# Two of eight token tiles of a product-key retrieval FFN read the expert table as 128 blocks instead of gathering rows

## The reference

```python
q = (xb @ w_query).astype(jnp.float32).reshape(T, PEER_HEADS, 2, PEER_HALF)
scores = jnp.einsum('thpd,hpkd->thpk', q, sub_keys.astype(jnp.float32))
s_top, i_top = lax.top_k(scores, PEER_TOPK)
...
gate = jax.nn.softmax(best, axis=-1)
u_e = expert_down[idx]
v_e = expert_up[idx]
act = jax.nn.gelu(jnp.einsum('thkd,td->thk', u_e, xb).astype(jnp.float32), approximate=False)
return jnp.einsum('thk,thkd->td', (gate * act).astype(xb.dtype), v_e)
```

## Time and profile before

| | |
|---|---|
| median of 3 runs | 2949.64 us (2945.9 to 2950.95) |
| profiled execution | 2951.25 us, its span 2949.5 us |
| busy share PE, DVE, ACT, POOL | 67%, 65%, 41%, 39% |
| DMA | 1181.83 MB, 401 GB/s mean over the span |
| granted TensorE clock, mean | 0.70 of 2.4 GHz |

### The profile page before, as it was taken

How to read it: one execution, slowest core, us unless ns; L and a number is a source line. 1 busy time by engine, 2 the same in 40 slices (tenths; PEclk the granted TensorE clock), 3 DMA queues, 4 the chain that set the end, 5 groups by cost and what they waited for, 6 DMA issues and landing times.

```text
span 2949.5 us, 37543 instructions
## 1 busy us (share of the span) xinstructions
PE 1973.1 (67%) x12770; PEld 899.5 (30%) x12770; DVE 1914.2 (65%) x4707; ACT 1205.3 (41%) x3855; POOL 1148.5 (39%) x1032
## 2 busy tenths in 40 slices
PE   5788888887977466666665656566666666566553
PEld 4454453443534122232322312132222223232110
DVE  4776656665766366677576766677576766666544
ACT  1245444354454243444344443444344444444333
POOL 0043333333444244444444444444444444444332
PEclk9888987988988567666567557665666656666555
DMA  9599999999999999999999999999999999999997
GB/s 404 198 372 402 371 387 395 384 417 389 420 418 372 381 419 420 421 411 421 420 421 421 410 420 419 418 406 421 420 413 420 409 415 418 414 409 417 421 421 293
DMA packets 176213, 1181.83 MB, mean 401 GB/s; under 512 B 19731, under 2 KB 28947, under 8 KB 42774
## 3 DMA queue, kind: packets, MB, share of 16 engines
q0 software_dynamic: 147456, 1073.81, 88.9%
q1 hardware_dynamic: 28566, 105.63, 9.2%
HBM read 1170.98 MB, written 8.39 MB: 400 GB/s over the span
## 4 chain that ended last, share of the span: by engine, by line
DMA 52%; PE 23%; DVE 13%; ACT 7%; issue 3%; SPq 1%; POOL 1%; DVEq 0%; ACTq 0%; POOLq 0%
DMA work<-experts,expert_rows 40%; DMA weights<-experts,expert_rows 9%; PE ps_sum L750 7%; DVE work L1294 5%; PE ps_small L719 4%; PE ps_m L668 3%; PE ps_wide L694 2%; PE ps_m L632 2%; PE ps_m L612 2%; ACT weight L931 1%; DMA work<-w_ada 1%; ACT diag L936 1%; DMA h_next<-x_scratch 1%; DVE weights L1294 1%; ACT act_out L929 1%
## 5 line engine op out<-in xcount | busy, mean ns | idle before, releaser
L564 POOL DMA_INDIRECT work<-experts,expert_rows x836 | 933.0, 1116 | 1470.0 <-PE ps_sum L750 1295.1
L1294 DVE CUSTOM_DVE_ANT_0 work<-work 128x1024 f32<-128x1024 f32 x836 | 1020.7, 1223 | 666.8 <-DMA work<-experts,expert_rows 665.6
L750 PE MATMUL ps_sum<-work,diag 128*32 128x256 f32 x6688 | 750.0, 534 | 674.3 <-ACT diag L936 670.9
L929 ACT ACTIVATE act_out<-act_in 128x1 f32<-128x1 f32 x1024 | 207.5, 203 | 1228.1 <-DVE act_in L1294 1224.8
L750 PEld LDWEIGHTS ps_sum<-work,diag 128*32 128x32 f32 x6688 | 154.6, 127 | 1162.6 <-ACT diag L936 1095.3
L936 ACT ACTIVATE diag<-const,weight 128x32 f32<-128x32 f32 x1024 | 329.1, 321 | 33.6
L1294 DVE CUSTOM_DVE_ANT_0 weights<-weights,work 128x1024 f32<-128x1024 f32 x188 | 230.1, 1224 | 153.3 <-DMA weights<-experts,expert_rows 152.9
L564 POOL DMA_INDIRECT weights<-experts,expert_rows x188 | 212.5, 1130 | 299.6 <-PE ps_sum L750 289.7
L931 ACT ACTIVATE weight<-gate,act_out 128x1 f32<-128x1 f32 x1024 | 301.7, 295 | 33.2
L750 PE MATMUL ps_sum<-weights,diag 128*32 128x256 f32 x1504 | 176.1, 555 | 203.8 <-ACT diag L936 196.4
L694 PE MATMUL ps_wide<-h_cur,const 32*128 32x512 f32 x260 | 211.4, 904 | 0.8 <-ACT work L903 0.8
(11 more groups left out here) (159 smaller groups left out, 1717.6 us busy)
## 6 DMA issues: line engine op xcount, KB each, us to landing
work<-sides SPq DMA_DIRECT2D x68, 576.0 KB, 8.1
work<-w_ada SPq DMA_DIRECT2D x12, 2048.0 KB, 23.8
work<-experts,expert_rows POOLq DMA_INDIRECT x836, 16.2
weights<-sides SPq DMA_DIRECT2D x12, 576.0 KB, 36.8
weights<-w_in SPq DMA_DIRECT2D x3, 2048.0 KB, 17.8
x_buf<-x SPq DMA_DIRECT2D x8, 512.0 KB, 11.2
weights<-w_out SPq DMA_DIRECT2D x2, 2048.0 KB, 37.0
x_scratch<-h_buf SPq DMA_DIRECT2D x8, 512.0 KB, 7.8
```

Of the source, the lines that this page charges most:

```text
L564: nc.gpsimd.indirect_dma_start(ring[x.ring], None, experts, bass.IndirectOffsetOnAxis(ap=rows_flat[:, x.column:x.column + 1], axis=0),).th ...
L750: last = nc.tensor.matmul(ps_sum[quarter(c), x.group, :], diag[:, x.ring, :], ring[x.ring][:, D + c * QCOLS:D + (c + 1) * QCOLS], start=x. ...
L929: nc.scalar.activation(act_out[:, s:s + 1], act_in[:, s:s + 1], ACT.Gelu).then_inc(s_gelu, 1)
L1294: nc.vector.tensor_tensor_reduce(down, down, h2_spread[x.segment % 2], 1.0, 0.0, ALU.mult, ALU.add, act_in[:, x.g % TURN:x.g % TURN + 1]). ...
```

## The change

**What it does.** Tiles 2 and 3 (`DENSE`) no longer gather. The six other tiles (`LEGS`) keep their 128 slots each, 768 in all. For the two tiles the 16384 experts are read once, as 128 blocks of 1.05 MB (all experts with the same second key; a plain DMA from an array laid out for it, issued by POOL into the same ring). A block takes 8 matmuls of 256 columns for the down products of all 256 tokens (`down`), a Gelu over 128 x 256 (`gelu_block`), a multiplication with the map (`gate_block`) and 4 matmuls of 512 columns (`up`), which add into four banks. Block b stands at slot 494 + b x 254 / 128, so that about every two slots hold one, up to slot 750.

**The map of gates** has one number for each of the 256 tokens and 16384 experts, 16.8 MB. For each token POOL makes two one-hot rows with the token's 128 choices on the partitions (`make_onehots`, two operations of 128 columns), PE multiplies them (`map_bank`), ACT copies four tokens at a time (`copy_map`), SP stores 16 tokens at a time in pieces of 512 bytes (`store_map`) and reads the map back in 16 parts of 1.05 MB (`load_map`). This is placed at slots 324 to 388 and 430 to 494.

**What else moves.** The ring gets 13 buffers from slot 296 on (6 before that). All 128 sides are streamed, none is held. The turns stand closer: 26 of the 32 begin before slot 494. Steps 4, 11, 12 and 13 of a turn use one wide DVE operation where there were two or four. The mixer ends at slot 293. The mixer's tiles now share one piece of memory, that the map and the blocks use afterwards. After the last block, at slot 752 and 757, DVE finishes the two dense tiles (`dense_end`).

```diff
+LEGS = (0, 1, 4, 5, 6, 7)
+DENSE = (2, 3)
+LAST_SLOT = len(LEGS) * SLOTS
+BLOCKS = KEYS
+DENSE_TOKENS = len(DENSE) * P
+
+
 RING_MIX = 6
-RING = 8
-MIX_TILES = 2
-LATE_SLOT = 268
-LATE_ORDER = (6, 7, 4, 5, 0, 1, 2, 3)
+RING = 13
+LATE_SLOT = 296
+LATE_ORDER = tuple(range(RING_MIX, RING)) + tuple((LATE_SLOT + i) % RING_MIX for i in range(RING_MIX))
+DIAGS = 8
 
...
-MIX_AT = {1: -MIX_HEAD, 2: 31, 3: 70, 4: 109, 5: 150, 6: 190, 7: 230}
+MIX_AT = {1: -MIX_HEAD, 2: 34, 3: 76, 4: 132, 5: 174, 6: 216, 7: 259}
...
+TURN_AT = {(0, 0): None, (0, 1): 2, (0, 2): 22, (0, 3): 42, (1, 0): 70, (1, 1): 88, (1, 2): 106, (1, 3): 126,
+           (2, 0): 175, (2, 1): 192, (4, 0): 209, (4, 1): 226, (2, 2): 243, (4, 2): 260, (4, 3): 277, (2, 3): 294,
...
-ROUTE_STEPS = 19
-EXP_SLOT, MOVE_SLOT = 11, 19
-SIDES_BEFORE = (20, 15, 10, 5)
-ROUTE_AT = [None, 2, 28, 50, 74, 98]
-for _t in range(1, TILES):
-    ROUTE_AT += [SLOTS * _t + s for s in (2, 28, 68, 94)][:2 if _t == TILES - 1 else 4]
...
-
-BATCHES = [((0,), (1,), (2,), (3,))] + [((0, 1), (2, 3))] * (TILES - 1)
...
+MAP_KEYS = 8
+MAP_PARTS = KEYS // MAP_KEYS
+MAP_STORE = 16
+MAP_BANK = 4
+MAP_BANKS = P // MAP_BANK
+
+TURN_CHOICES_AT = [TURN_AT[t, PAIRS - 1] + MOVE_SLOT + 1 for t in DENSE]
+MAP_MADE_AT = [g + 14 for g in TURN_CHOICES_AT]
+MAP_TOKENS = 2
+MAP_BACK = 6
+
+DENSE_FROM, DENSE_SLOTS = 494, 254
+DOWN, GELU, GATED_D, UP = 1, 2, 3, 4
+DENSE_END = 752
 
...
+class Block:
+
+
+    def __init__(self, b):
+        self.b, self.g = b, DENSE_FROM + b * DENSE_SLOTS // BLOCKS
...
+def fill_ring(table, blocks):
+
+    fills, last, late = [0] * RING, [None] * RING, 0
     for x in table:
-        fills[x.ring] += 1
-        x.fill, x.before = fills[x.ring], last[x.ring]
-        last[x.ring] = x.g
-    return table, starts
+        for y in [x] + [block for block in blocks if block.g == x.g]:
+            if x.g < LATE_SLOT:
+                y.ring = x.g % RING_MIX
+            else:
+                y.ring, late = LATE_ORDER[late % RING], late + 1
+            fills[y.ring] += 1
+            y.fill, y.before = fills[y.ring], last[y.ring]
...
+            def store_map(i, n):
+                banks = MAP_STORE // MAP_BANK
+                if n % banks == banks - 1:
+                    store = (MAP_BANKS * i + n) // banks
+                    sp.wait_ge(s_map_sb, MAP_BANKS * i + n + 1)
+                    sp.dma_start(map_dram[:, :, store, :].rearrange("a p x -> p a x"),
+                                 map_store[store % 2]).then_inc(s_map_st[store % 2], 16)
+
+            def load_map(part):
+                if part < 2:
+                    for i in range(2):
+                        sp.wait_ge(s_map_st[i], 16 * (DENSE_TOKENS // MAP_STORE // 2))
+                else:
+                    sp.wait_ge(s_gated_d, MAP_KEYS * (part - 1))
...
+            def make_onehots(i, token):
+
+                bank = (P * i + token) // MAP_BANK
+                if token % MAP_BANK == 0:
+                    pool.wait_ge(s_numbers, 16)
+                    pool.wait_ge(s_choices, i + 1)
+                    if bank >= 2:
+                        pool.wait_ge(s_map_ps, bank - 1)
+                first, second = (onehot[bank % 2][:, e, token % MAP_BANK, :] for e in range(2))
+                nc.gpsimd.tensor_scalar(first, numbers, choices_t[:, 0, token:token + 1], None, ALU.is_equal)
+                nc.gpsimd.tensor_scalar(second, numbers, choices_t[:, 1, token:token + 1],
+                                        choices_t[:, 2, token:token + 1], ALU.is_equal, ALU.mult).then_inc(s_onehot, 1)
+
+            for x in TABLE:
+                gather(x)
+                for i, at in enumerate(MAP_MADE_AT):
+                    for token in range((x.g - at) * MAP_TOKENS, (x.g - at + 1) * MAP_TOKENS):
+                        if 0 <= token < P:
+                            make_onehots(i, token)
+                for block in blocks_at(x.g):
+                    wait_free(pool, block)
+                    nc.gpsimd.dma_start(ring[block.ring], blocks[block.b]).then_inc(s_row[block.ring], 16)
...
+            def map_bank(i, n):
+
+                bank = MAP_BANKS * i + n
+                pe.wait_ge(s_onehot, MAP_BANK * (bank + 1))
+                if bank >= 2:
+                    pe.wait_ge(s_map_sb, bank - 1)
+                else:
+                    pe.wait_ge(s_x1, TILES)
+                for token in range(MAP_BANK):
+                    last = nc.tensor.matmul(ps_map[bank % 2][:, token * KEYS:(token + 1) * KEYS],
+                                            onehot[bank % 2][:, 0, token, :], onehot[bank % 2][:, 1, token, :],
+                                            start=True, stop=True)
+                last.then_inc(s_map_ps, 1)
+
+            def down(block, queries_done, sides_done):
+
+                pe.wait_ge(s_row[block.ring], 16 * block.fill)
+                pe.wait_ge(s_q_sb, queries_done)
+                pe.wait_ge(s_score_sb, sides_done)
+                if block.b:
+                    pe.wait_ge(s_gelu_d, block.b)
+                else:
+                    pe.wait_ge(s_h2_d, 2)
+                    pe.wait_ge(s_wide_sb, WIDE_USE["turn", DENSE[1], 1] + 1)
+                weights_of = ring[block.ring][:, 0:D].rearrange("p (k e) -> p k e", k=KC)
+                for k in range(KC):
+                    last = nc.tensor.matmul(ps_d, weights_of[:, k, :], h2_d[:, k, :], start=(k == 0), stop=(k == KC - 1))
+                last.then_inc(s_down, 1)
+
+            def up(block):
+                pe.wait_ge(s_gated_d, block.b + 1)
+                if block.b == 0:
+                    pe.wait_ge(s_map_sb, MAP_BANKS * len(DENSE))
+                for i in range(len(DENSE)):
+                    for half in range(2):
+                        last = nc.tensor.matmul(ps_dense[i][half], gated_d[block.b % 2][:, i * P:(i + 1) * P],
+                                                ring[block.ring][:, D + half * HALF:D + (half + 1) * HALF],
+                                                start=(block.b == 0), stop=(block.b == BLOCKS - 1))
+                last.then_inc(s_block, 1)
...
+                for block in blocks_at(x.g - DOWN):
+                    down(block, queries_done, sides_done)
+                    downs += 1
+                for block in blocks_at(x.g - UP):
+                    up(block)
...
+            def copy_map(i, n):
+                bank, banks = MAP_BANKS * i + n, MAP_STORE // MAP_BANK
+                store = bank // banks
+                act.wait_ge(s_map_ps, bank + 1)
+                if store >= 2:
+                    act.wait_ge(s_map_st[store % 2], 16 * (store // 2))
+                at = bank % banks * MAP_BANK * MAP_KEYS
+                target = map_store[store % 2][:, :, at:at + MAP_BANK * MAP_KEYS].rearrange("p a (t k) -> p t a k", k=MAP_KEYS)
+                nc.scalar.copy(target, ps_map[bank % 2][:, :].rearrange("p (t a k) -> p t a k", t=MAP_BANK, k=MAP_KEYS)
+                               ).then_inc(s_map_sb, 1)
+
+            def gelu_block(block):
+                act.wait_ge(s_down, block.b + 1)
+                if block.b >= 2:
+                    act.wait_ge(s_gated_d, block.b - 1)
+                nc.scalar.activation(gelu_d[block.b % 2], ps_d, ACT.Gelu).then_inc(s_gelu_d, 1)
...
+            def gate_block(block):
+
+                part = block.b // MAP_KEYS
+                if block.b % MAP_KEYS == 0:
+                    dve.wait_ge(s_map_ld[part % 2], 16 * (part // 2 + 1))
+                if block.b >= 2:
+                    dve.wait_ge(s_block, block.b - 1)
+                dve.wait_ge(s_gelu_d, block.b + 1)
+                nc.vector.tensor_tensor(gated_d[block.b % 2], gelu_d[block.b % 2],
+                                        map_part[part % 2][:, :, block.b % MAP_KEYS], ALU.mult).then_inc(s_gated_d, 1)
+
```

More of the change, by code:

```diff
@@ L187, with wide_uses, map_banks @@
 WIDE_USE, WIDE_AT = wide_bank_uses()
+def wide_uses(g):
+    return [what for what, at in WIDE_AT.items() if at == g and g >= 0]
+def map_banks(g, after):
+    found = []
+    for i, at in enumerate(MAP_MADE_AT):
+        tokens = (g - at - after) * MAP_TOKENS
+        found += [(i, n) for n in range(MAP_BANKS) if tokens <= MAP_BANK * n + MAP_BANK - 1 < tokens + MAP_TOKENS]
+    return found
 def build(nc, x, w_ada, b_ada, columns, w_in, w_pool, pool_scale, w_spatial_t, b_spatial, w_out, g_norm2,
-          sides, experts, g_final, constants, first_constants, x1_dram, out):
+          sides, experts, blocks, g_final, constants, first_constants, key_numbers, x1_dram, map_dram, gate2_dram, out):
     with ExitStack() as ctx:
@@ new lines, in copy_choices, with place_dense_h2 @@
+            def copy_choices(i):
+                act.wait_ge(s_wide_ps, WIDE_USE["choices", i] + 1)
+                if i:
+                    act.wait_ge(s_onehot, P * i)
+                else:
+                    act.wait_ge(s_x1, TILES)
```

(10 more changed lines are left out.)

592 lines of the change are left out of this document (383 added, 209 removed), and 2 rows, old and new, of the table TURN_AT.

## The result

The changed kernel takes **3155.22 us** (median of 4 runs, 3150.28 to 3161.92) against 2950.3 us for the kernel before (4 runs, 2945.9 to 2955.26). The ratio is 1.070, with an interval of 1.0669 to 1.0722: 7.0% slower. The profiled execution took 3161.92 us, of which 3160.1 are its span. The forecast was 3005 us with a range up to 3090: the direction is right, the size is not, and the result lies 65 us above the range.

What follows compares the result with a forecast made beforehand. DMA bytes were taken to bound the kernel, with PE taking over in the dense stretch: 1700 (up to slot 494) + 1255 (dense stretch) + 48 (end) + 1.75 around the span = 3005 us; own range 2957 to 3050, wider range 2900 to 3090.

Steps and rivals of the forecast that it cites:

- The bytes: Whole program's DMA: gathers gone, blocks, sides and map added, sum -149 us; about 2802 us if bytes bounded it everywhere.
- the dense stretch: Slots 494 to 750: PE needs 1220 us against DMA's 1044, with waits 1255 us, 9.9 us for two slots.
- Up to slot 494: Start to slot 494: DMA stays the bound, 1568 + 57 + 60 + 15 = 1700 us.
- the stores at 60: Before slot 494: storing the map in pieces of 512 bytes costs 60 us, between 43 and 86.
- 15 for short pieces: Mixer's part and pause at slot 296: short PE work leaves DMA without a free buffer, 15 us, between nothing and 40.
- POOL's one-hots: Four per slot over 128 slots, 0.25 to 0.4 us each; 2.1 to 2.7 us a slot against 3.3 of transfers, cost nothing.
- The rival: POOL becomes the bound in the one-hots: at 0.7 us each, 3.9 us a slot, 80 us, total 3085 us; chance 0.13.
- the stalls: Dense stretch: waits of PE beyond its work, 35 us in all, for Gelu and gates; 0 to 60 allowed.
- The rival of the shorter pitch: `down` and `up`: long matmul runs go faster, block 7.2 us, stretch 1200, kernel 2950; chance 0.17 of 2905 to 2957.
- The end: Slots 750 to the end: last 17 slots at DVE's pace, dense tiles' end, last leg's chain; 48 us.
- Bytes still bound the dense stretch: Dense stretch: PE's work fits in 8.2 us for two slots, kernel 2802 us, up to 2900; chance 0.13.
- The blocks at a low clock: Dense stretch: PE's clock falls to 1.2 GHz at the blocks and the stretch takes twice as long; chance 0.02.

Runs made afterwards that it cites:

- the kernel of the prices: Separate kernel, no part of the layer: 48 operations of 128 columns of each of four kinds on POOL alone, under DVE dots, and on DVE; 342.45 us.

## Why the prediction was wrong, step by step

- **The bytes.** Right: the queues moved 71 MB less, and once PE was relieved of half of `down` the dense stretch ran at 1062 us, forecast as 1044.
- **Up to slot 494, without POOL.** 1700 forecast, 1720 by the run without one-hots. The parts, 38 sides, the stores at 60 and 15 for short pieces, weren't separated. The stores are rather too dear in it (38 to 57 by the run that doubled them), so something else of 23 to 42 us is missing; its cause stays open. One reading was wrong and cost nothing: PE's 1036 + 155 us belong to the time from 148 us on, 1537 us and not 1685, so that PE was to be busy for 77% of it and not 71%.
- **POOL's one-hots: the step that failed.** "I take 0.25 to 0.4 with one … Cost nothing." They cost 176 us. The nearest rows were two fills, and from 0.2 us for a fill I came to at most 0.4 for an operation that reads a tile, takes a value per partition from a second one and, in half of the cases, does two operations. Its price alone is 0.58 and 0.77 us; that and 1.14 for the gather make 3.8 us for a slot, already over the 3.3 us of its transfers, some 69 us for 128 slots. The rest is what DVE's dots add, for which no row of before had a case. The rival had the mechanism and 0.7 us for one, near the price alone; with the mean of 0.89 us its own formula gives 4.7 us a slot and 128 x 1.4 = 179 us. The chance of 0.13 and the end of the range at 3090 were set by its one price: the upper end should have been worked out with operations that sit out dots, since the rival's own text named dots on DVE as what holds POOL up.
- **The dense stretch.** PE as the bound, at 97% busy, a clock of 0.99 and a DMA share of 0.94 (0.85 forecast): right. The size, 1208 for 1255, is off mostly by one term: a block is 7.25 us, not 7.64, 50 us over 128 blocks. With 7.25 the sum for PE is 1170 us, and the window says 1171.4 busy; so the stalls are 38 us, where I took 35. In these runs of eight an instruction of 512 columns takes 3.63 / 8 = 0.454 us, for the 0.478 of the earlier trace rows, which came from four in a row. The time that the prediction took from the Trainium skill, page "TensorE: Matmul & The Clock Gate", section "Wait — 56ns, not 53.3ns?", is 0.432 us, an estimate; the trace lies midway between it and the row. The rival of the shorter pitch, 7.2 us, had the right block; "it decides under 9.4 us for a pair of slots" came out with 1208 / 128 = 9.44.
- **The end.** 58 us for 48; DVE's last dots, the dense tiles' end and the last leg's chain weren't separated.
- **The rivals otherwise.** Bytes still bound the dense stretch: no, but nearly, at 0.94. The blocks at a low clock: no, 0.99.

The sum of the misses: 176 (POOL) + 20 (the rest up to slot 494) - 50 (block) + 3 (stalls) + 10 (end) = 159, against the 157 us between forecast and profiled execution. The forecast had the direction right, "slower", and this was not POOL's doing alone: without the one-hots the kernel takes 2978 us, still 0.9% slower than before and inside the stated range. That it lies only 27 us under the forecast is in part luck, since the dense stretch was too dear by 54 us against that run (1255 and 1201) while the rest was too cheap by 28.

## What to carry to other kernels

Elementwise work put on an engine that "only waits" must be priced per instruction on that engine: one that stands in front of the issue of transfers sets the pace of all of them once its slot is longer than the transfer, and two tokens of 1.8 us each were more here than the 2.2 us that its transfers left beside the gather's issue. When an engine's queue alternates between a pipeline's step and side work, look at whether the side work waits for something that stands behind the same slot's step on another engine. Here two buffers didn't keep such a ring from forming (more of them weren't tried), and one step moved ahead opened it (101 us). And when work is made PE-bound in order to save bytes, spread it over as many slots of transfers as its inputs allow: with the same bytes saved, that decided whether the kernel won (with the ring open, blocks over 261 slots 0.2% slower than before, over 293 slots 1.5% faster).

## What was not expected of the hardware

A POOL operation of 128 columns under back-to-back dots of DVE takes 3.2 to 5 times its own time (0.58 to 2.0, 0.77 to 2.9, 0.39 to 1.25, 0.24 to 1.18 us), and one that starts under a single dot ends about 0.7 us after it, where its own price is 0.8. The dots lose less: 1.22 to 1.30 us beside compares and copies and 1.42 to 1.47 beside the product in the kernel of the prices, 1.33 and 1.40 in the changed kernel's rows. And on POOL a compare with a value per partition is dearer than a product of two tiles (0.58 against 0.39 us), on DVE it is not (0.20 for both). A matmul instruction of 512 columns in a run of eight takes 0.454 us, in a run of four 0.478.
